# Low halves of 68 weight slabs made by VectorE instead of GpSimd in a two-block transformer

## The reference, cut to what matters

```
for l in range(DEPTH):                       # 2 layers, 16 + 512 = 528 positions, 1024 wide
    h = rms_norm(x, norm_mix[l])
    proj = h @ w_in[l]
    u_pool, q, k, v, p_rw, gate_logits = jnp.split(proj, IN_SPLITS, axis=-1)
    b_pool = pool_mixer(u_pool, pool_w[l], pool_scale[l])
    b_da = diff_attention(q, k, v, lam, lambda_init, da_subln[l])
    b_rw = rwkv7_mixer(p_rw, ...)
    up = jnp.einsum('blnc,ncd->blnd', jnp.stack([b_pool, b_da, b_rw], axis=2), w_branch[l])
    gates = sigmoid(gate_logits.reshape(B, L, 3, 1024))
    x = x + sum(gates * up, axis=2) @ w_out[l]
    x = x + conv_glu_ffn(rms_norm(x, norm_ffn[l]), ffn_up[l], ffn_conv[l], ffn_down[l])
```

## Time and profile before

| | |
|---|---|
| median of 3 runs | 2704.22 us (2700.59 to 2706.65) |
| profiled execution | 2706.09 us, span 2703.9 us |
| granted TensorE clock, mean | 0.998 |
| busy: TensorE, VectorE, ACT, GpSimd | 2646.0, 1823.1, 1134.5, 353.1 us |
| share of the span | 98%, 67%, 42%, 13% |

### The profile page before, as it was taken

One profiled execution on the slowest core, in us unless ns is written; L12 is line 12 of the kernel. 1 busy time (PEld: TensorE's weight loads), 2 busy tenths in 40 slices (PEclk: granted clock), 3 DMA queues, 4 the chain that ended last, 5 costly groups with the idle time before them and its releaser, 6 DMA issues.

```text
span 2703.9 us, 55964 instructions
## 1 busy us (share of the span) xinstructions
PE 2646.0 (98%) x24551; PEld 2417.2 (89%) x24551; DVE 1823.1 (67%) x2786; ACT 1134.5 (42%) x1844; POOL 353.1 (13%) x217
## 2 busy tenths in 40 slices
PE   8999999999999999999999999999999999999998
PEld 7988998999999999988898899999987788877886
DVE  7744345556888746934335555888836998887887
ACT  6333335524333324423324624333323345466664
POOL 1211122230111000211122221111100000010001
PEclk9999999999999999999999999999999999999999
DMA  4211322364343343211232263334332322399996
GB/s 149 75 50 35 98 84 65 118 195 148 125 135 124 133 139 108 86 50 35 77 93 77 75 191 122 118 125 141 116 115 75 107 81 99 144 384 386 396 392 253
DMA packets 114203, 373.19 MB, mean 138 GB/s; under 512 B 13072, under 2 KB 14240, under 8 KB 113568
## 3 DMA queue, kind: packets, MB, share of 16 engines
q1 hardware_dynamic: 88848, 303.97, 33.2%
q10 hardware_dynamic: 18592, 41.92, 4.4%
q0 software_dynamic: 6512, 23.62, 2.4%
HBM read 336.44 MB, written 31.94 MB: 136 GB/s over the span
## 4 chain that ended last, share of the span: by engine, by line
PE 84%; DVE 10%; ACT 3%; DMA 1%; issue 1%; POOL 0%; SPq 0%; DVEq 0%; ACTq 0%; POOLq 0%
PE PS L316 83%; DMA RING<-wts 1%; DVE ARENA L1218 1%; DVE ARENA L846 1%; DVE HR L482 1%; DVE RINGR L311 1%; ACT ARENA L408 0%; PE PS L3270 0%; PE PS L1425 0%; DVE ARENA L848 0%; DVE H L492 0%; DVE ARENA L813 0%; ACT ARENA L410 0%; DVE ARENA L815 0%; DVE WR L3259 0%
## 5 line engine op out<-in xcount | busy, mean ns | idle before, releaser
L316 PE MATMUL PS<-HR,HIGHR 128*128 128x264 f32 (+1 forms) x2976 | 845.1, 284 | 0.0
L316 PEld LDWEIGHTS PS<-HR,HIGHR 128*128 128x128 f32 x2976 | 561.3, 189 | 0.8
L316 PE MATMUL PS<-XR,HIGHR 128*128 128x264 f32 (+2 forms) x1760 | 546.1, 310 | 6.0 <-ACT STAGE L612 5.3
L300 ACT CAST HIGHR<-RING 128x1024 fp32r<-128x1024 f32 (+2 forms) x340 | 330.7, 977 | 289.9 <-DMA RING<-wts 111.1
L316 PE MATMUL PS<-XR,RINGR 128*128 128x264 f32 (+1 forms) x1568 | 445.5, 284 | 0.0
L316 PE MATMUL PS<-HH,HIGHR 128*128 128x264 f32 (+2 forms) x1472 | 424.4, 288 | 2.9 <-DVE RINGR L311 1.4
L316 PE MATMUL PS<-HH,RINGR 128*128 128x264 f32 (+2 forms) x1472 | 421.4, 286 | 0.0
L311 DVE TENSOR_TENSOR RINGR<-RING,HIGHR 128x1024 fp32r<-128x1024 f32 (+2 forms) x272 | 311.3, 1149 | 118.0 <-ACT HIGHR L300 118.0
L316 PEld LDWEIGHTS PS<-XR,HIGHR 128*128 128x128 f32 x1760 | 331.8, 189 | 39.4 <-issue 19.4
L316 PE MATMUL PS<-ARENA 64*64 64x64 f32 (+10 forms) x7946 | 296.9, 240 | 12.3 <-DVE ARENA L1218 2.9
L316 PEld LDWEIGHTS PS<-XR,RINGR 128*128 128x128 f32 x1568 | 296.5, 189 | 0.0
(11 more groups left out here) (446 smaller groups left out, 5134.4 us busy)
## 6 DMA issues: line engine op xcount, KB each, us to landing
RING<-wts SPq DMA_DIRECT2D x324, 512.0 KB, 3.6
ARENA<-wmoe SPq DMA_DIRECT2D x204, 512.0 KB, 6.8
RING<-wts SPq DMA_DIRECT2D x52, 256.0 KB, 3.1
gates<-STAGE ACTq DMA_DIRECT2D x48, 264.0 KB, 4.3
ARENA<-gates ACTq DMA_DIRECT2D x48, 264.0 KB, 2.9
ys<-RING ACTq DMA_DIRECT2D x16, 512.0 KB, 7.1
RING<-wts SPq DMA_DIRECT2D x16, 384.0 KB, 3.1
ys<-STAGE POOLq DMA_DIRECT2D x8, 512.0 KB, 6.1
```

The lines of the kernel that those rows point to most:

```text
L300: e.copy(k.highR[:, hs, 0:n], k.ring[:, i % NRING, 0:n]).then_inc(*k.s["hi"].done(i))
L316: return e.matmul(out, lhsT, rhs, start=start, stop=stop, skip_group_check=True)
```

## The change

Three words change: the slabs that were given to GpSimd are given to VectorE.

```diff
@@ gate_pe
     sl = k.slabs.use(("gate", l, i), [("w_in", (l,), 0, 8, 3840 + n * 1024 + m * 128, 128)],
-                     ("gate_pe", (l, i, 1)), lo="lo_pool")
+                     ("gate_pe", (l, i, 1)), lo="lo_dve")
@@ pool_in_pe
-    sl = k.slabs.use(("pool", l, g), [("w_in", (l,), 0, 8, g * 128, 128)], ("pool_pe", (l, g, "in", 1)), lo="lo_pool")
+    sl = k.slabs.use(("pool", l, g), [("w_in", (l,), 0, 8, g * 128, 128)], ("pool_pe", (l, g, "in", 1)), lo="lo_dve")
@@ inputs_pe
     slab = lambda i: k.slabs.use(("lin", l, i), [("w_in", (l,), 0, 8, (16 + STEPS[i]) * 128, 128)],
                                  ("lin_pe", (l, "in", i)) if i else ("ahead_pe", (("mix", l), 7)),
-                                 lo="lo_pool" if 6 <= i <= 11 else "lo_dve")
+                                 lo="lo_dve")
```

## The result

The change makes the kernel slower: 2718.07 us (median of 5 runs, 2715.60 to 2727.37) against 2704.22, 13.85 us more; the ratio is 1.0055, with a 95% interval of 1.0044 to 1.0066. 2717.7 was predicted.

What follows compares the result with a forecast made beforehand. The prediction took TensorE, busy for 98% of the span, to bound the kernel. Five terms sum to 6.75 us a layer, 13.5 for two layers, on a median of 2704.2: 2717.7 us, range 2707 to 2726.

Steps and rivals of the forecast that it cites:

- the five places: Input stage's end, core tiles 1 to 3, after the core: low parts waiting in line cost 6.75 us a layer; chance 0.72.
- end of the input stage, L821 and L1201: Third gate's low part before L1201 delays TensorE 1.62 us, less 0.25 of L821's wait: +1.4 us a layer, up to 1.9.
- tile 1, C and A4: Core: low part before copy C (L1215) delays copy A4, which TensorE awaits: +1.3 us a layer, between -1.06 and +1.9.
- tile 2: Core: low part before L1222 delays it and the L1211 that TensorE awaits: +1.5 us a layer.
- tile 3: Core: low part between two L1211 delays the second, for which TensorE already waits: +1.15 us a layer.
- gate 11: After the core: low part behind the third L1355 delays this gate's matmuls: +1.4 us a layer, between 1.15 and 1.5.
- all eight holds go: Input stage: VectorE loses eight holds, some 15 us, gets eight low parts, 9.2 us, so reaches the last step earlier.
- What was costed at nothing: Low parts of input slabs 6 to 11, the core's others, and those in attention and behind it: zero cost.
- The first rival: Holds decide, waits in line are hidden: TensorE's 3.7 us of waits for L1201, L1215, L821 go; 2700.5 us, chance 0.14.
- The holds: VectorE instructions blocked while GpSimd runs a low part: about 2.4 us goes for every 1.15 us of work VectorE gets.
- One sign: Whole kernel: TensorE's waits behind VectorE grow by some 14 to 17 us in all.

Runs made afterwards that it cites:

- Experiments 3, 4 and 5: Changed kernel with, in turn, two places reordered on VectorE, low parts asked one piece later, ACT's high parts one slab ahead: 2711.01, 2707.70, 2711.98 us.
- experiment 1: Kernel before, with only the 12 low parts of input-stage slabs 6 to 11 moved to VectorE: 2700.65 us, ratio 0.9990.
- experiment 6: Changed kernel with input-stage slabs 6 to 11 back on GpSimd, gates and pools (56 low parts) on VectorE: 2717.55 us, ratio 1.0050.
- experiment 2: Changed kernel with the 20 low parts of core gates 2 to 11 back on GpSimd, 48 left on VectorE: 2700.25 us, ratio 0.9990.
- experiment 7: Changed kernel with two places reordered on VectorE and low parts asked one piece later, all 68 on VectorE: 2698.82 us, ratio 0.9983.
- the first four experiments: Four versions (input stage only; core gates back; two places reordered; low parts one piece later), timed beside the kernel before, whose median was 2703.07 us.

## Why the prediction was right

By its own steps. TensorE has the same 24551 instructions in the same order in both traces, so each one's start can be set against its start before. The lag of the changed kernel grew as follows at the five places (lag ahead of the place to lag behind it, first and second layer):

| place | predicted | measured, layer 1 | measured, layer 2 |
|---|---|---|---|
| end of the input stage, L821 and L1201 | +1.4 | 0.14 to 1.22: +1.1 | 6.59 to 7.67: +1.1 |
| tile 1, C and A4 | +1.3 | 2.70 to 4.23: +1.5 | 6.15 to 7.65: +1.5 |
| tile 2 | +1.5 | 3.95 to 5.46: +1.5 | 5.58 to 7.08: +1.5 |
| tile 3 | +1.15 | 5.45 to 6.59: +1.1 | 7.07 to 8.23: +1.2 |
| gate 11 | +1.4 | 6.58 to 7.95: +1.4 | 8.09 to 9.46: +1.4 |
| sum | 6.75 | 6.6 | 6.6 |

Both layers give 13.2 us where 13.5 was predicted; the medians differ by 13.85. The rule by which each place was priced, end of the high part plus one low part minus the old start of what stands behind, held at all five, in tile 1 for C and not for the copy A4 that the term was taken from. That the sum is as close as 0.15 us a layer is in part luck, since two terms were off in opposite directions. Experiments 3, 4 and 5 took the terms away through the order of VectorE's or ACT's program, without taking work from VectorE.

- *End of the input stage*, 0.3 too high: the delay at L1201 was 1.62 us, as predicted, but without the holds TensorE gained 0.55 ahead of it, not 0.25, 0.42 of it at L821. The reason given for VectorE's being early, that all eight holds go, was wider than needed: with the first six gone (experiment 1) or the last two (experiment 6) it is early too.
- *Tile 1*, 0.2 too low: the price was taken from A4's copy, but TensorE did not wait for A4 at all. It lost 1.70 us waiting for C and 0.64 for L1218, had its gates' products still to do then, and came to A4 after the copy was there.
- *What was costed at nothing* was nothing: 48 low parts on VectorE in experiment 2 gave 2700.25 us, and in attention the lag of the changed kernel does not grow (8.08 us at 380 us of before, 7.95 at 490).
- *The first rival*, that only the holds count, was out for this order of work and right for another: experiment 7, in which no low part holds TensorE up at the five places, gives back what it foresaw and a little more, 2698.8 against 2700.5. The rule of the Trainium skill, "SBUF — State Buffer", section "Who interferes with whom", describes a real effect: the held two-input instructions of the earlier trace rows are short without GpSimd's low parts, and so are those of the earlier trace rows. It does not say what VectorE has to wait for in their place.
- *The holds* were read too large. VectorE's instructions other than L311 take 77.4 us less with the change (1622.6 to 1545.1 us), 1.14 us for each low part moved and not 2.4: about a third of the low parts on GpSimd held nothing. Nor is every instruction held that reads SBUF alone: at 393.80 in the trace of before, 0.95 us into a low part of 2.37 us, the reciprocal L1611 (16x2) takes 0.15 us. And L786 takes 0.49 us unheld, not 0.7.
- *One sign* came out smaller than named: TensorE's waits behind VectorE grew by 12.0 us (23.8 to 35.8), not by 14 to 17. Those for L821 and some for low parts outside of the five places shrank.

The two profiled executions differ by 9.5 us only (2715.60 against 2706.09), less than the 13.2 of the five places. In the lags the rest is seen outside of these: the changed kernel's lag grows by 1.5 us in the first layer's tile 0, where its clock was low, and shrinks by 1.5 and 2.1 us in the second layer's core, where that of before was low (of the 2.1, some 1.4 go with the clock); and 1.1 us are shed at the end of the first layer, where TensorE waited 0.89 us for a low part before and 0.22 after. The execution of before that was profiled is one of the slower of its runs. Among the runs beside the first four experiments and those of the change, at the same mean clock of 0.998, ten of before have a median of 2701.3 us and two of the change 2715.6, 14.3 apart.

## What to carry to other kernels

Moving a piece of work to an engine with room for it can cost time without adding to that engine's busy time: what counts is which wait the work brings along, and what stands behind it in that engine's order. Price each place by the time at which the input is made, not by the engine's load; then either give the wait to an engine that has nothing behind it, or ask for the work one step after its input is made. An engine that another holds up is worth freeing only where something waits for it, and here that was 1.7 us a layer (experiment 7, in TensorE's lags).

## What the runs showed that had not been expected

The spread between runs of one kernel goes for the most part with the granted clock. Runs of before between 2697.3 and 2707.6 us have mean clocks from 0.999 to 0.996. In the trace it is a few short stretches, often around the core's tile 0, where TensorE has done many small products without a pause and then falls from its upper level (2.4 GHz) to the lower one (1.2 GHz) in the midst of work, and soon rises again. Windows of the changed kernel (length, busy time and count of each engine, granted clock, DMA share, GB/s):

```profile
142.00:144.00 2.00, 2.00 (x39) 1.55 (x36) 0.56 (x2) 0.00 (x0) 0.00 (x0) 1.00 0.00 0
144.00:146.00 2.00, 2.00 (x65) 1.93 (x65) 0.00 (x0) 0.00 (x0) 0.00 (x0) 1.00 0.03 8
146.00:148.00 2.00, 2.00 (x14) 2.00 (x15) 0.00 (x0) 0.00 (x0) 0.00 (x0) 0.80 0.00 0
148.00:150.00 2.00, 2.00 (x22) 1.76 (x23) 0.00 (x0) 0.39 (x1) 0.00 (x0) 0.50 0.00 0
150.00:152.00 2.00, 2.00 (x32) 1.97 (x29) 0.42 (x1) 0.21 (x1) 0.00 (x0) 0.84 0.76 193
152.00:154.00 2.00, 2.00 (x87) 1.83 (x88) 0.47 (x1) 1.07 (x2) 0.00 (x0) 1.00 0.56 213
```

The engine was busy throughout, and 1.5 us were lost against the same stretch of before, which ran at the full clock. In the profile of before the same happened in the second layer, from 1176 to 1180 us, and not in the first; a second fall there, from 1214 to 1217 us, came after TensorE had been busy for only 1.16 and 1.34 of 2 us in two windows. What makes the clock fall is not shown. So two single profiles can differ by a few us where the change has no part in it, and places are better compared by TensorE's waits than by spans.
